# Forgetting attention with unnormed projections by groups of four heads, attention between half slabs, output by rows, and the gate sums in the bias

## What is computed

```python
def fox_mixer(x, w_in, f_bias, w_out):            # x is rmsnorm(x, gain) here
    proj = x @ w_in                                # 1024 x (3*1024 + 16)
    q, k, v = ...                                  # 16 heads of 64
    q = q * (hd ** -0.5)
    log_f = log_sigmoid(proj[..., 3 * 1024:] + f_bias)
    c = cumsum(log_f, axis=1)                      # per head, over tokens
    s = einsum('bhqd,bhkd->bhqk', q, k) + c[..., None] - c[:, :, None, :]
    p = masked_softmax(s, pos[None, :] <= t[:, None])
    o = einsum('bhqk,bhkd->bhqd', p, v)
    return o @ w_out                               # added to x
```

## Time and profile before

| | us |
|---|---|
| runs shown, median of 3 | 4648.8 (4642.49 to 4649.01) |
| profiled execution | 4639.7 |
| its span, first to last instruction | 4638.3 |
| TensorE busy in the span | 4368.8 (94%) |
| VectorE busy | 3061.2 (66%) |
| ScalarE busy | 1963.5 (42%) |
| mean granted TensorE clock | 0.944 of full |

### The profile page before, as it was taken

How to read it: one execution, slowest core, us unless ns; L and a number is a source line. 1 busy time by engine, 2 the same in 40 slices (tenths; PEclk the granted TensorE clock), 3 DMA queues, 4 the chain that set the end, 5 groups by cost and what they waited for, 6 DMA issues and landing times.

```text
span 4638.3 us, 71997 instructions
## 1 busy us (share of the span) xinstructions
PE 4368.8 (94%) x30860; PEld 4008.8 (86%) x30860; DVE 3061.2 (66%) x4396; ACT 1963.5 (42%) x2499; POOL 105.6 (2%) x109
## 2 busy tenths in 40 slices
PE   8989999899988999889898999999998999999998
PEld 7778888787887888778786999999998699999998
DVE  6567674676676766566537799648753379964864
ACT  5345453554545544454325443342343344234233
POOL 0000000000011000010000000000000000000000
PEclk9989999899999999889967999999998699999999
DMA  5424454254532545325330453353453145345343
GB/s 213 181 88 164 175 188 167 94 183 163 184 134 80 189 173 185 118 90 183 132 110 28 160 185 120 141 187 128 146 192 118 46 159 185 112 155 183 118 155 145
DMA packets 94702, 679.30 MB, mean 146 GB/s; under 512 B 11296, under 2 KB 11952, under 8 KB 12848
## 3 DMA queue, kind: packets, MB, share of 16 engines
q1 hardware_dynamic: 91152, 662.74, 39.5%
q0 software_dynamic: 1024, 7.61, 0.4%
q10 hardware_dynamic: 2208, 4.34, 0.3%
HBM read 671.48 MB, written 3.17 MB: 145 GB/s over the span
## 4 chain that ended last, share of the span: by engine, by line
PE 83%; DVE 13%; ACT 2%; issue 1%; POOL 1%; DMA 0%; ACTq 0%; DVEq 0%; POOLq 0%; SPq 0%
PE psum L615 20%; PE psum L544 14%; PE psum L545 14%; PE psum L546 14%; PE psum L616 10%; PE psum L1035 3%; DVE slab_low L1413 2%; DVE room L1942 1%; DVE room L1677 1%; PE psum L696 1%; PE psum L698 1%; DVE x L1530 1%; DVE room L1958 1%; PE psum L566 1%; DVE room L1940 1%
## 5 line engine op out<-in xcount | busy, mean ns | idle before, releaser
L1413 DVE TENSOR_TENSOR slab_low<-slab,slab_high 128x2048 fp32r<-128x2048 f32 x632 | 1449.5, 2294 | 817.9 <-ACT slab_high L1054 815.1
L1054 ACT ACTIVATE slab_high<-slab 128x2048 fp32r<-128x2048 f32 x632 | 1204.1, 1905 | 516.0 <-PE psum L616 267.8
L544 PE MATMUL psum<-h_parts,slab_high 128*128 128x256 f32 x3488 | 1011.9, 290 | 71.5 <-DVE h_parts L1456 69.4
L615 PE MATMUL psum<-h_parts,slab_high 128*128 128x512 f32 x2816 | 1002.5, 401 | 40.3 <-DVE h_parts L1491 40.3
L545 PE MATMUL psum<-h_parts,slab_high 128*128 128x256 f32 x3488 | 998.6, 286 | 0.0
L546 PE MATMUL psum<-h_parts,slab_low 128*128 128x256 f32 x3488 | 998.1, 286 | 0.0
L616 PE MATMUL psum<-h_parts,slab_low 128*128 128x256 f32 x2816 | 792.4, 281 | 0.0
L544 PEld LDWEIGHTS psum<-h_parts,slab_high 128*128 128x128 f32 x3488 | 681.6, 195 | 82.1 <-issue 73.5
L615 PEld LDWEIGHTS psum<-h_parts,slab_high 128*128 128x128 f32 x2816 | 533.7, 190 | 173.7 <-issue 19.7
L545 PEld LDWEIGHTS psum<-h_parts,slab_high 128*128 128x128 f32 x3488 | 681.8, 195 | 2.0 <-issue 1.9
L546 PEld LDWEIGHTS psum<-h_parts,slab_low 128*128 128x128 f32 x3488 | 681.1, 195 | 0.0
(11 more groups left out here) (261 smaller groups left out, 4872.7 us busy)
## 6 DMA issues: line engine op xcount, KB each, us to landing
slab<-in_up SPq DMA_DIRECT2D x176, 1024.0 KB, 4.8
slab<-in_keys_up SPq DMA_DIRECT2D x128, 1024.0 KB, 4.8
slab<-in_keys_down SPq DMA_DIRECT2D x128, 1024.0 KB, 4.8
slab<-in_down SPq DMA_DIRECT2D x88, 1024.0 KB, 4.8
slab<-in_w_in SPq DMA_DIRECT2D x16, 1024.0 KB, 4.8
slab<-in_wq SPq DMA_DIRECT2D x16, 1024.0 KB, 4.8
slab<-in_w_pw SPq DMA_DIRECT2D x12, 1024.0 KB, 4.8
slab<-in_w_qkv SPq DMA_DIRECT2D x12, 1024.0 KB, 4.8
```

Of the source, the lines that this page charges most:

```text
L544: nc.tensor.matmul(out, lhs[0], rhs[0], start=first, stop=False, **options)
L615: nc.tensor.matmul(out, lhs[0], rhs, start=first, stop=False, **options)
L1054: nc.scalar.activation(k.high[m % PARTS][:, 0:width], k.slabs[m % RING][:, 0:width], ACT.Copy).then_inc(k.rounded.up())
L1413: nc.vector.tensor_tensor(k.low[m % RING][:, 0:width], k.slabs[m % RING][:, 0:width], k.high[m % PARTS][:, 0:width], ALU.subtract).then_in ...
```

## The change

- The stage enters like the feed-forward stage: unnormed input times gain, squares added on GpSimd (`add_squares`, taken out of `ffn`), sums after the first slab. Besides the sums over channels in rows, one column per query tile is made, so that the reciprocal root exists along tokens (for k) and along partitions (for q and v). q stays unscaled, its factor goes into the score's scale; k is scaled by VectorE as it leaves its bank, v by ScalarE.
- The slabs come as q, k, v of four heads, four times. Gates are computed from `x` with a weight that has the gain in it, after the second slab's first half.
- The work goes in ticks of half a slab (`project_half`, the products of a half of `project_slab`). After the half come, in ticks 6 to 13, two products that spread -c over all queries of a pair of heads; VectorE adds the causal mask and keeps the result (`decay`) as the bias of the items. The query's own term is left out, as it is the same for a whole row of a softmax. Items start in the ticks of `v.starts` and are worked on after the halves, with one buffer each for scores (banks 4 and 5), transposes (6) and values (7).
- The output matrix comes by rows: a slab holds two chunks of input rows for all outputs, and its products accumulate in banks 0 to 3, as for the experts. `x` is added at the end, in four steps.

`early_input` on VectorE makes the low part as L1491 does. `shift`, `normalise` and ScalarE's steps are those of the old attention, with a scale per token. The core of the diff:

```diff
+    v.q, v.keys, v.v, v.o = k.carve(DC, T), k.carve(DC, T), k.carve(TT, D), k.carve(DC, T)
+    attention_views(k, v)
+    v.decay = k.carve(NH, P + T)
     v.w_f, v.f, v.soft, v.c = k.carve(DC, NH), k.carve(T)[0:NH, :], k.carve(T)[0:NH, :], k.carve(T)[0:NH, :]
...
+    v.scales = k.carve(TT)
+    v.jobs = [(dst[:, 2 * j:2 * j + 2, :], 0) if dst is not v.v else (v.v[:, :, j * T:(j + 1) * T], T) for j in range(4) for dst in (v.q, v.keys, v.v)]
+    v.items = [dict(tile=i, pair=pair, q=v.q[:, pair, :], k=v.keys[:, pair, :],
+                    v=lambda b, kt, pair=pair: v.v[:, kt, (2 * pair + b) * HD:(2 * pair + b + 1) * HD],
+                    bias=v.decay[:, 2 * pair:2 * pair + 2, P * i:P * i + P * (i + 1)], scale=v.scales[:, i:i + 1])
+               for pair in range(NP) for i in range(TT)]
+    v.starts = [8, 9, 10, 11, 12, 13, 14, 15, 18, 19, 20, 21, 24, 24, 25, 25]
...
+    def mixed_half(self, v, j, e):
+        if e == 0:
+            self.pair = self.take()
+        high, low = self.pair
+        nc.tensor.wait_ge(k.mixed_ready.sem, k.mixed_ready.at(2 * j + e + 1))
+        mixed = v.mixed[:, 2 * j + e, 0, :], v.mixed[:, 2 * j + e, 1, :]
+        for c in range(DC):
+            cols = slice(e * D + c * P, e * D + (c + 1) * P)
+            mm = self.product(k.banks[c // 2][:, (c % 2) * T:(c % 2 + 1) * T], (high[:, cols], low[:, cols]), mixed,
+                              j == 0 and e == 0 and c % 2 == 0, j == DC // 2 - 1 and e == 1, skip_group_check=True)
+        if e == 1:
+            mm.then_inc(k.slab_done.up())
...
+    def sums(self, v):
+        nc.tensor.wait_ge(k.squares_added.sem, k.squares_added.at(3))
+        nc.tensor.wait_ge(k.move.sem, 16)
+        ones = k.const("ones")
+        for a in range(2):
+            nc.tensor.matmul(k.banks[7][:, 0:T], ones, v.squares[:, a, :], start=(a == 0), stop=(a == 1))
+        for i in range(TT):
+            for a in range(2):
+                mm = nc.tensor.matmul(k.banks[7][:, T + i:T + i + 1], v.squares[:, a, i * P:(i + 1) * P], ones[:, 0:1], start=(a == 0), stop=(a == 1))
+        mm.then_inc(k.summed.up())
...
+    def attend(self, v, tick, inputs):
+        for n in starting(v, tick - 3):
+            it = v.items[n]
+            i = it["tile"]
+            nc.tensor.wait_ge(k.settled.sem, k.settled.at(n + 1))
+            if n >= 1:
+                nc.tensor.wait_ge(k.collected_act.sem, k.collected_act.at(n))
+            for e in range(2):
+                for kt in range(i + 1):
+                    mm = nc.tensor.matmul(k.banks[7][HD * e:HD * e + HD, 0:P], it["v"](e, kt),
+                                          v.probs_t[:, n % 3, e, kt * P:(kt + 1) * P], start=(kt == 0), stop=(kt == i))
+            mm.then_inc(k.valued.up())
+        for n in starting(v, tick - 2):
+            i = v.items[n]["tile"]
+            nc.tensor.wait_ge(k.normed.sem, k.normed.at(n + 1))
+            if n >= 1:
+                nc.tensor.wait_ge(k.settled.sem, k.settled.at(n))
+            for e in range(2):
+                for kt in range(i + 1):
+                    at = (2 * e + kt) * P
+                    mm = nc.tensor.transpose(k.banks[6][:, at:at + P], v.probs[:, n % 5, e, kt * P:(kt + 1) * P], k.const("ident"))
+            mm.then_inc(k.turned.up())
+        for n in starting(v, tick):
+            it = v.items[n]
+            i, keys = it["tile"], P * (it["tile"] + 1)
+            inputs(it)
+            if n >= 1:
+                nc.tensor.wait_ge(k.biased.sem, k.biased.at(n))
+            for e in range(2):
+                rows = slice(HD * e, HD * e + HD)
+                mm = nc.tensor.matmul(k.bank_pairs[2][:, e, 0:keys], it["q"][rows, i * P:(i + 1) * P], it["k"][rows, 0:keys], start=True, stop=True)
+            mm.then_inc(k.scored.up())
...
-        self.norm(v)
-        self.qkv(v)
-        nc.tensor.wait_ge(k.small.sem, k.small.at(1))
-        for n in range(DC):
-            mm = nc.tensor.matmul(k.banks[6][0:NH, 0:T], v.w_f[:, n, :], v.h[:, n, :], start=(n == 0), stop=(n == DC - 1))
-        mm.then_inc(k.gates_made.up())
-        nc.tensor.wait_ge(k.evacuated.sem, k.evacuated.at(len(v.jobs)))
-        nc.tensor.wait_ge(k.opened.sem, k.opened.at(1))
-        self.attention(v)
-        self.out_project(DC)
+        self.stage_enters(False)
+        def inputs(it):
+            group = it["pair"] // 2
+            nc.tensor.wait_ge(k.evacuated.sem, k.evacuated.at(2 * group + 2))
+            nc.tensor.wait_ge(k.columns_scaled.sem, k.columns_scaled.at(group + 1))
+        for tick in range(2 * len(v.jobs) + DC):
+            n, half = tick // 2, tick % 2
+            if n < len(v.jobs):
+                if half == 0 and n >= 3:
+                    if n % 3 == 1:
+                        nc.tensor.wait_ge(k.columns_scaled.sem, k.columns_scaled.at(n // 3))
+                    else:
+                        nc.tensor.wait_ge(k.evacuated.sem, k.evacuated.at(2 * (n // 3) - (1 if n % 3 == 0 else 0)))
+                self.project_half(n, half, k.banks[n % 3], v.jobs[n][1])
+            else:
+                if n == len(v.jobs) and half == 0:
+                    nc.tensor.wait_ge(k.evacuated.sem, k.evacuated.at(8))
+                    nc.tensor.wait_ge(k.columns_scaled.sem, k.columns_scaled.at(4))
+                    nc.tensor.wait_ge(k.decayed.sem, k.decayed.at(NP))
+                self.mixed_half(v, n - len(v.jobs), half)
+            if tick == 1:
+                self.sums(v)
+            if tick == 2:
+                nc.tensor.wait_ge(k.gates_made.sem, k.gates_made.at(1))
+                for c in range(DC):
+                    mm = nc.tensor.matmul(k.banks[3][0:NH, 0:T], v.w_f[:, c, :], k.x[:, c, :], start=(c == 0), stop=(c == DC - 1))
+                mm.then_inc(k.gates_made.up())
+            if 6 <= tick < 6 + NP:
+                pair = tick - 6
+                if pair == 0:
+                    nc.tensor.wait_ge(k.opened.sem, k.opened.at(1))
+                else:
+                    nc.tensor.wait_ge(k.decayed.sem, k.decayed.at(pair))
+                for b in range(2):
+                    hd = 2 * pair + b
+                    mm = nc.tensor.matmul(k.banks[3][:, b * T:(b + 1) * T], k.const("npick")[:, hd:hd + 1].to_broadcast([NH, P]), v.c,
+                                          start=True, stop=True)
+                mm.then_inc(k.decay_made.up())
+            self.attend(v, tick, inputs)
...
+    def early_input(self, v, gain):
+        if k.slab_done.start:
+            nc.scalar.wait_ge(k.slab_done.sem, k.slab_done.start)
+        for c in range(DC):
+            ready, value = k.x_ready(c // 2)
+            nc.scalar.wait_ge(ready.sem, value)
+            nc.scalar.activation(k.h[:, c, 0, :], k.x[:, c, :], ACT.Copy, scale=k.vec(gain, c)).then_inc(k.h_rounded.up())
+        for j in range(DC // 2):
+            nc.scalar.activation(v.square[:, 2 * j:2 * j + 2, :], k.x[:, 2 * j:2 * j + 2, :], ACT.Square).then_inc(k.squared.up())
...
+    def attend(self, v, tick):
+        for n in starting(v, tick - 4):
+            it = v.items[n]
+            nc.scalar.wait_ge(k.valued.sem, k.valued.at(n + 1))
+            nc.scalar.activation(v.o[:, it["pair"], it["tile"] * P:(it["tile"] + 1) * P], k.banks[7][:, 0:P],
+                                 ACT.Copy).then_inc(k.collected_act.up())
+            if it["tile"] == 1:
+                nc.scalar.wait_ge(k.collected_act.sem, k.collected_act.at(n + 1))
+                nc.scalar.activation(v.mixed[:, it["pair"], 0, :], v.o[:, it["pair"], :], ACT.Copy).then_inc(k.mixed_rounded.up())
...
+        self.early_input(v, "l1_attn_norm")
+        for tick in range(2 * len(v.jobs) + DC + 1):
+            n, half = tick // 2, tick % 2
+            if half == 0 and n < len(v.jobs) + DC // 2:
+                self.round_slab()
+            if half == 0 and 1 <= n <= len(v.jobs) and (n - 1) % 3 != 1:
+                dst, by_token = v.jobs[n - 1]
+                bank = k.banks[(n - 1) % 3].rearrange("p (a t) -> p a t", a=2)
+                nc.scalar.wait_ge(k.slab_done.sem, k.slab_done.at(n))
+                if by_token:
+                    nc.scalar.wait_ge(k.rooted.sem, k.rooted.at(2))
+                    for i in range(TT):
+                        copy = nc.scalar.activation(dst[:, i, :], bank[:, i, :], ACT.Copy, scale=v.rstd[:, T + i:T + i + 1])
+                else:
+                    copy = nc.scalar.activation(dst, bank, ACT.Copy)
+                copy.then_inc(k.evacuated.up())
+            if tick == 2:
+                self.root(v.rstd)
+            if tick == 4:
+                nc.scalar.wait_ge(k.kept.sem, k.kept.at(1))
+                nc.scalar.activation(v.soft, v.f, ACT.Abs).then_inc(k.absd.up())
+                nc.scalar.wait_ge(k.absd.sem, k.absd.at(1))
+                nc.scalar.activation(v.soft, v.soft, ACT.Exp, scale=-1.0).then_inc(k.exps.up())
+                nc.scalar.wait_ge(k.exps.sem, k.exps.at(1))
```

(57 more changed lines are left out.)

162 lines of the change are left out of this document (109 added, 53 removed).

## The result

Four runs of the changed kernel have a median of 4589.2 us (4578.0 to 4592.5), four of the kernel before 4645.7 us (4633.0 to 4649.0). The ratio is 0.9879, 95% interval 0.9853 to 0.9905: faster by 56 us, where 4577 (4556 to 4621) had been forecast. The profiled execution took 4591.1 us, 48.6 less than that of before.

The account below looks back on a forecast made before the run. TensorE, holding 83% of the chain of waits, was taken as the bound. Entry 3.3, pacing 0.5, GpSimd 2.1, work 127.3, waits 13.2 and clock 6 gave 152.4, with exit 154.6 against 221.3 us: 4577 us, range 4556 to 4621.

Parts of the forecast that it names:

- Waits: TensorE's waits in the changed stage: 3.3 us at entry, 2.1 for GpSimd's squares, 13.2 together from gates on.
- tick 24: Output by rows needs banks 0 to 3 at once, so it waits 1.8 us for the last evacuation.
- hand-overs: Ticks 24 to 28, two items each on single buffers: six waits of about 0.5 us, 3.1 together.
- TensorE's work at full clock: Stage's halves 92.2, sums 1.4, gates 3.6, decay 7.3 and attention 22.8 us: 127.3 in all.
- pacing: First half of the first slab is paced by VectorE's low parts at 0.41 us each: 0.5 us added.
- Clock: Drops to 1.2 GHz behind waits among the halves: four of 3 us each, half of that time lost, 6 us.
- Exit: After the stage's last output matmul, x is added in four steps before the next stage: cost 2.3 us.
- DMA: Loads of w_f and the slabs land before they are needed, so they cost nothing.
- Rival 1: Clock oscillates, half of the 23 shared ticks at 1.2 GHz: 4621 us, a quarter of them 4596; chance 0.13.
- Rival 2: Clock stays low from the gates at tick 2 on: 113 us more, 4690, slower; chance 0.04.
- Rival 3: Attention items don't fit between halves, 1.5 us of wait in each of 20 ticks: 4607 us; chance 0.12.
- Rival 4: Stage gains more: no cost from drops or hand-overs, 4568 us, without decay waits 4562; chance 0.68 together with the forecast.

Follow-up runs that it names:

- the mended kernel: Changed kernel with decay additions first, one item a tick, last evacuation before rounding, sums and decay a half later: 4565.6 us, again 4561.2.
- bias alone: Kernel before with only the 16-row score products replaced by 16 decay products that VectorE adds to the mask: 4596.5 us, ratio 0.9891.
- attention apart: All attention items run behind the last projection instead of among halves: 4594.6 us on the changed kernel, 4571.8 on the mended kernel.
- three mends: Changed kernel with decay additions before the slab step, one item a tick, and last bank evacuated before the slab's rounding at tick 24: 4570.0 us.

## Why the prediction was right, and where it was off

The forecast of 4577 lay 12 below the median, in its range. Some 10 of the 12 are the stage, and 2 the kernel before, whose median came out at 4645.7 where the forecast took 4643.7. What was done away with, and which waits take its place, it had right; what the interleaving is worth in this gain it did not ask (last point). By its own steps, with the stage at 162.3 where 152.4 was summed:

- **Waits** (entry, GpSimd, gates, decay, tick 24, hand-overs): 18.6 summed, 18.4 measured. Entry 3.1 for 3.3; GpSimd 1.4 for 2.1; gates 1.6 for 1.8; decay 5.2 for 6.5, with no wait in tick 7 where 1.0 was put; tick 24 1.8 for 1.8; hand-overs 5.4 for 3.1, the one mis-sized term: of the six one took 1.95 us, where an item's values waited for ScalarE's copy of the item before out of their one bank (L1399), and the others 0.69 on average where 0.5 was put. They were found in the places that VectorE's and ScalarE's written order gives, which is why they could be costed before they existed.
- **TensorE's work at full clock**: 127.3 with 0.5 of pacing, against 132.9 (the mended kernel's 134.4 less some 1.5 for its one stretch at 1.2 GHz). Short by 5.1. One term was missing: a half that stands between float32 products takes 3.06 us from start to start, 0.10 more at its first matmul and 0.08 more behind its last, where one among its own kind takes 2.88; there are some 23 such halves: 4. The other was small: a pair of decay products 1.06 us, not 0.9, so 1.3.
- **Clock**: 6 us for four drops of 3 us, half of each lost. The changed kernel had five stretches at 1.2 GHz, three of 3.4 us and two of 6.8, 23.9 us together (the same sum in seven stretches of 3.4 when it was run again); its busy time is 143.9 - 132.9 = 11 longer for them. Short by 5. The rows below show one tick of it: the last full-clock matmul, the wait, in whose last quarter of a microsecond the clock fell (3543.6), and a matmul of the next half, 0.41 long where 0.28 was the rule before.

```profile
3541.29 0.28 PE L552 MATMUL psum<-slab_high,h_parts 128*128 128x256 f32 x1
3543.81 2.07 PE L979 MATMUL psum<-room,consts 16*128 16x256 f32 x4 [2.24 <-DVE room L2011]
...
3547.54 0.41 PE L551 MATMUL psum<-slab_low,h_parts 128*128 128x256 f32 x1
```

- **Exit** 2.0 for 2.3. **DMA** nothing, as said.
- **Rivals.** Rival 1, half of the shared ticks at 1.2 GHz: their mean granted clock was 0.91, so it is wrong as sized, though right in kind, for behind the entry the stretches of low clock follow waits of 1.3 to 2.2 us on a bank. Its price was too high as well: a matmul that starts every 0.12 us at full clock starts every 0.21 at the low one, so a half wholly at 1.2 GHz costs 2.2 us more, not 2.9. The Trainium skill ("TensorE: Matmul & The Clock Gate", section "A second HAM failure mode: psum-queue depth-cycling") blames small idles between groups that cycle through PSUM banks; the trace agrees at these waits, and not at the six hand-overs, one of 1.95 us among them, after which the clock stayed up; with the decay additions first, the same hand-over had a drop behind it. And idle time is not the only way down: with the gate terms as products the clock fell three times with no wait ahead. Rival 2 (low clock from the 16-column and 16-row products on) did not come about: in the mended kernel all eight pairs of decay products among halves ran in 1.06 us each at full clock, and even the gate terms as products let the clock come back each time. Rival 3 (the items don't fit) was the true place of the hand-overs, at 5 us and not at 30. Rival 4's time (4562 to 4568, with no drops, hand-overs and decay waits) came about, but only with the mends.
- **The signs it named.** Missed: the last output matmul came 162.3 us after the last expert matmul, not 150 to 156, and the clock fell to 0.73 in one stretch of 12 us (3538 to 3550) where over 0.9 was put for each. Met, or nearly: 1.4 us of wait for GpSimd where about 2 was put, 1.6 for the gates, 2.2 in one of the two decay ticks and 1.7 in the other where 2 to 3 was put, 12.2 us to the next stage's first projection. What would have made it wrong (0.5 to 0.7 over the shared ticks, waits over 1 us for scores or transposes) did not come; the longest of these was 0.92.
- **What the prediction did not ask**: how the gain divides. It spoke of the attention as the prize, and of hiding it. In the stage, before to bias alone -51.7, from there to the kernel with early entry and output by rows -5.2 (of which the exit gives 2.0 back), interleaving -1.9 or so; in the medians of the batches it is -50.2 for the bias, nothing to be seen for entry and output (this kernel, too, is 50 below the kernel before), and -8.9 for interleaving. By either count all the rest of the diff, the early entry, the slabs by groups, the halves and the items between them, bought some 5 to 9 of the 56 to 59 us, because the attention freed of its 16-row products needed 34.5 us and kept TensorE busy in 30.5.

The four mends give 4561 to 4566 us against 4586 to 4589, 20 to 25 us below the changed kernel and about 80 below that of before: the best version here.

## What to carry to other kernels

Take the small-row products out first, and time that alone: without them an attention of 104 us took 51, the bias made in their place included. Moving their term into a bias that VectorE adds once cost 14 us alone and 8.5 among halves. Work that is laid between other work must not bring its own waits: write each engine's order of a tick down, put whatever frees a single bank ahead of long steps that nothing awaits soon (here L1590's 2.3 us), and let each product wait for no more inputs than it reads. A wait of one to two microseconds on TensorE costs its length, and often some 1.5 us more in the low clock behind it (a half of 4.5 us where 3.06 is due), or twice that where the stretch lasts 6.8 us.

## What the runs showed of the hardware that was not expected

- A half of 24 matmuls of 256 columns (float32r) takes 3.06 us between float32 products and 2.88 among its own kind: 0.10 us at the change to it and 0.08 at the change back.
- TensorE's clock can fall while TensorE never waits: three times in 102 us when every score carried its 16-row products (0.92 over that stretch, 0.51 over 7 us of it). With no such products in the scores and no waits (the four mends, twice) it fell nowhere behind the entry. So both a wait and these products can bring a drop, and neither does each time; what decides was not separated.
- The clock of an attention alone is not set by the attention's kind. In the kernel before it stood at 0.52 over 104 us with TensorE never idle, and came back only for the last 4; without the 16-row products the same scores, transposes and values came back to full clock by themselves after 28 us (bias alone), or after 14 or 27 us at 1.2 GHz (attention apart, in the changed kernel, 0.76 over 34.5 us, and in the mended one, 0.65 over 39). What differs between them is what ran ahead of it and how long TensorE waited there; which of the two decides was not separated.
- A stretch at low clock can be free. The first two halves took 7.3 to 7.5 us and the wait for GpSimd behind them 1.35 to 1.55 where the stage began at low clock, and 6.2 with a wait of 2.67 in the two kernels where it did not (gate terms as products; three mends): 8.8 us each time, since GpSimd's additions (4.66 us for the last two, as in the earlier trace rows) set the end. It costs only where TensorE is what the others wait for.
